# Moving the hardware loop of an expert pipeline by one pair, and splitting one expert's weight transfers

## The reference

```python
def moe_ffn(h, w_router, b_router, w_gu, b_gu, w_down, b_down):
    logits = t @ w_router + b_router                 # t: 256 tokens x 1024
    top_vals, top_idx = lax.top_k(logits, 4)         # 4 of 32 experts
    combine = scatter(softmax(top_vals))             # 256 x 32
    for e in range(32):
        gu = t @ w_gu[e] + b_gu[e]                   # 1024 x 2048 weights, 8 MB
        gate = min(gu[:, :1024], 7); lin = clip(gu[:, 1024:], -7, 7)
        act = gate * sigmoid(1.702 * gate) * (lin + 1)
        y = act @ w_down[e] + b_down[e]              # 1024 x 1024 weights, 4 MB
        out = out + combine[:, e:e+1] * y
    return out
```

## Time and profile before

| | |
|---|---|
| median of three runs | 1018.23 us |
| profiled execution | 1017.21 us |
| its span | 1015.3 us |
| PE busy | 957.4 us (94%) |
| DVE busy, ACT busy | 286.4 us, 134.3 us |
| moved by DMA | 419.63 MB, 413 GB/s over the span |
| PE waiting for gate/up weights | 42.9 us in 14 waits |

### The profile page before, as it was taken

How to read it: one execution, slowest core, us unless ns; L and a number is a source line. 1 busy time by engine, 2 the same in 40 slices (tenths; PEclk the granted TensorE clock), 3 DMA queues, 4 the chain that set the end, 5 groups by cost and what they waited for, 6 DMA issues and landing times.

```text
span 1015.3 us, 11590 instructions
## 1 busy us (share of the span) xinstructions
PE 957.4 (94%) x4807; PEld 416.8 (41%) x4807; DVE 286.4 (28%) x542; ACT 134.3 (13%) x215; POOL 10.2 (1%) x16
## 2 busy tenths in 40 slices
PE   8999999999998998989899898989899898999996
PEld 8978343434342432424243242424234342434332
DVE  5964522213121222122122112212211311222123
ACT  6825100000000010000001000000100000010002
POOL 0030000000000000000000000000000000000000
PEclk9999999999999998999999999999989998999998
DMA  9789999999999999999999999999999999999994
GB/s 322 274 374 378 387 424 423 427 429 427 430 431 430 431 432 431 425 430 429 432 431 434 431 428 426 431 432 434 432 432 429 426 429 431 434 432 432 421 424 197
DMA packets 28871, 419.63 MB, mean 413 GB/s; under 512 B 4276, under 2 KB 5960, under 8 KB 10888
## 3 DMA queue, kind: packets, MB, share of 16 engines
q1 hardware_dynamic: 28800, 419.16, 97.7%
q10 hardware_dynamic: 40, 0.01, 0.0%
HBM read 418.11 MB, written 1.05 MB: 413 GB/s over the span
## 4 chain that ended last, share of the span: by engine, by line
PE 57%; DMA 40%; DVE 2%; issue 0%; ACT 0%; SPq 0%; DVEq 0%
PE ps L1050 54%; DMA raw<-in_w_gu 37%; DMA raw<-in_w_down 4%; PE ps L1328 1%; PE ps L1383 1%; DVE woutl L774 1%; DVE biased L973 0%; PE ps L1057 0%; DMA cst<-in_consts 0%; PE ps L1225 0%; DVE acc L1029 0%; DVE outs L1032 0%; DVE uT L763 0%; DVE prT L796 0%; ACT junk L695 0%
## 5 line engine op out<-in xcount | busy, mean ns | idle before, releaser
L1050 PE MATMUL ps<-raw,xT 128*64 128x512 f32 x2032 | 472.2, 616 | 43.4 <-DMA raw<-in_w_gu 42.9
L1050 PEld LDWEIGHTS ps<-raw,xT 128*64 128x64 f32 x2032 | 143.2, 141 | 343.5 <-issue 282.7
L1050 PE MATMUL ps<-raw,actT 128*64 128x512 f32 x1024 | 232.3, 596 | 1.5 <-DMA raw<-in_w_down 1.3
L1050 PEld LDWEIGHTS ps<-raw,actT 128*64 128x64 f32 x1024 | 70.5, 137 | 135.3 <-issue 129.4
L973 DVE TENSOR_TENSOR biased<-ps,biasT 128x1024 f32<-128x1024 f32 x32 | 39.2, 1225 | 294.8 <-PE ps L1328 294.8
L651 ACT ACTIVATE gu<-ps 128x1024 f32<-128x1024 f32 x32 | 32.8, 1025 | 526.0 <-PE ps L1050 526.0
L990 DVE TENSOR_TENSOR acc<-ps,acc 128x512 f32<-128x512 f32 x60 | 38.8, 686 | 176.3 <-PE ps L1050 176.3
L874 DVE TENSOR_TENSOR xT<-ps,gT 128x512 f32<-128x512 f32 x32 | 22.1, 692 | 166.1 <-PE ps L1050 165.9
L1050 PE MATMUL ps<-ysc,dispT 64*128 64x512 f32 x256 | 65.5, 613 | 0.0
L1050 PEld LDWEIGHTS ps<-disp,h 128*128 128x128 f32 x512 | 58.4, 192 | 12.4 <-issue 12.2
L1050 PE MATMUL ps<-disp,h 128*128 128x128 f32 x512 | 61.7, 278 | 0.2 <-DVE disp L868 0.2
(11 more groups left out here) (163 smaller groups left out, 434.3 us busy)
## 6 DMA issues: line engine op xcount, KB each, us to landing
raw<-in_w_gu SPq DMA_DIRECT2D x55, 4096.0 KB, 33.4
raw<-in_w_down SPq DMA_DIRECT2D x62, 2048.0 KB, 31.4
raw<-in_w_gu SPq DMA_DIRECT2D x16, 2048.0 KB, 11.4
win<-in_w_in SPq DMA_DIRECT2D x15, 512.0 KB, 12.2
wout<-in_w_out SPq DMA_DIRECT2D x4, 1024.0 KB, 9.2
raw<-in_w_down SPq DMA_DIRECT2D x4, 1024.0 KB, 36.6
early<-in_w_gu SPq DMA_DIRECT2D x1, 2048.0 KB, 10.0
raw<-in_w_gu SPq DMA_DIRECT2D x2, 1024.0 KB, 6.0
```

The lines of the kernel that those rows point to most:

```text
L1050: return pe.matmul(out_, lhsT, rhs, start=start, stop=stop, skip_group_check=shared)
```

## The change

SP's and PE's loops run over other pairs. Pairs 0 and 1 are straight code, the loop runs four times over pairs 2 to 13, and pairs 14 and 15 are straight code. The call with `biases=True` is now that of pair 14, since pair 13 is in the loop. And pair 14 loads expert 30's gate/up weights by quarters of 2 MB, four transfers, where before it were two of 4 MB; the four semaphores of expert 1's quarters serve a second time (hence `uses=2`). The bytes and their order in the queue are as before.

```diff
 # SP
-            for third in range(3):
-                iteration(0, third)
-            with sp.Fori(1, triples) as j:
-                for third in range(3):
-                    iteration(j, third)
-            iteration(triples, 0)
-            iteration(triples, 1, small_next=last_loaded)
+            iteration(0, 0)
+            with sp.Fori(0, triples) as j:
+                iteration(j, 1)
+                iteration(j, 2)
+                iteration(j + 1, 0)
+            iteration(triples, 1, small=second_loaded, small_next=last_loaded)
             iteration(triples, 2, last=True)
 # PE
-            def gu_unit(half, c, s, count, pieces=None):
+            def gu_unit(half, c, s, count, pieces=None, uses=1):
...
-                        pe.wait_ge(pieces[c // 2], 16)
+                        pe.wait_ge(pieces[c // 2], 16 * uses)
...
-            def iteration(j, third, last, first=False, biases=False, pieces=None):
+            def iteration(j, third, last, first=False, biases=False, pieces=None, pieces_next=None, uses=1):
...
-                        gu_unit(0, k, buffer(j, third, 6 + k // 2), i + 1, third_loaded if first else None)
+                        gu_unit(0, k, buffer(j, third, 6 + k // 2), i + 1, pieces_next, uses)
...
-            iteration(None, 0, False, first=True, pieces=second_loaded)
+            iteration(None, 0, False, first=True, pieces=second_loaded, pieces_next=third_loaded)
             iteration(0, 0, False, pieces=fourth_loaded)
-            iteration(0, 1, False)
-            iteration(0, 2, False)
-            with pe.Fori(1, triples) as j:
-                for third in range(3):
-                    iteration(j, third, False)
-            iteration(triples, 0, False, biases=True)
-            iteration(triples, 1, False)
+            with pe.Fori(0, triples) as j:
+                iteration(j, 1, False)
+                iteration(j, 2, False)
+                iteration(j + 1, 0, False)
+            iteration(triples, 1, False, biases=True, pieces_next=second_loaded, uses=2)
             iteration(triples, 2, True, pieces=last_loaded)
```

## The result

The changed kernel took 1019.42 us, the median of 12 runs (1018.45 to 1022.41), beside 1017.76 us for the kernel before in 12 runs. The ratio is 1.0018, with a 95% interval of 1.0010 to 1.0025: 1.8 us slower, within the 0.3% that the prediction calls no change (the two medians lie 1.66 apart). The profiled execution took 1018.57 us with a span of 1016.6, where before it was 1017.21 and 1015.3. It is one of the shortest of the twelve, whose spans run from 1016.6 to 1020.6 with a median of 1017.6, so the 1.3 us between the two profiles need not be the 1.8 of the ratio.

A forecast was written before the change was run, and what follows sets the result against it. The prediction took weight transfers to bound the kernel until pair 14, then PE's own work. Its terms, +3.62 + 1.7 − 1.65 − 1.06 − 0.97 = +1.64, put the median of 1018.23 at 1019.9 us, range 1017.1 to 1022.4.

The forecast's parts named there:

- Biases, +3.62: Bias matmuls move from pair 13 to pair 14, ahead of its two short waits, and cost 3.62 us there.
- Low clock, +1.7: At pair 14's start, PE runs at low clock behind the longer wait and pays 1.7 us more.
- the 3.9 I gave: PE's wait ahead of pair 14 grows from 0.29 us to 3.9 us.
- the first rival: Long stretch of low clock at pair 14, price 3.0 us, and no gain from code: +3.9, 1022.1 us; chance 17%.
- Short waits taken up, −2.71: PE no longer waits 1.65 us for expert 30's second gate/up half, nor 1.06 us for its first down weights.
- Stream sooner, −0.97: Pairs 5 to 6 and 13 to 14 become loop turns without code loading, so weights come 0.97 us sooner.
- there I had 0.34: From pair 5 to 6, the distance falls from 58.78 to 58.44 us without code loading.
- Quarters, 0: Expert 30's gate/up weights in 2 MB transfers, issued one unit earlier at best, change the time by 0.
- Loop returns, 0: Returns at pairs 5, 8 and 11 are hidden behind waits for weights: cost 0, up to a few tenths without cover.
- the end on transfers: The end rests on transfers and PE takes up the biases: −0.97 to −1.58, 1016.7 to 1017.3 us; chance 8%.

## Why the prediction was right

Forecast were 1.64 us more; 1.8 were measured (1.0 to 2.5 by the interval). The mechanism held: the biases keep their price, a low clock comes behind the new wait, and the short waits take up part of both. That the sum came so close has luck in it. In the profile the sum was 0.34 too high, by the short waits; the terms of the clock and of the stream came near partly by chance, as the list shows; and beside the kernel with only the biases moved (1.0019) the stream's term cannot be seen in the changed kernel's time (1.0018). By its steps, against the profile:

- **Biases, +3.62.** Measured 16.56 − 11.24 − (5.35 − 3.65) = 3.62. Moving them alone gives the whole effect (1.0019).
- **Low clock, +1.7.** Measured 1.70 behind a wait of 3.39, and removed by filling that wait. The size was half luck: in the eight profiles in which pair 14 has a wait of over 3 us and no filler, four have the short stretch (5.24 or 5.35) and four the long (6.16 to 6.53). The wait was half a microsecond shorter than the 3.9 I gave, because I did not carry my own 0.63 us from the stream into it. In other executions the same term was 2.88 (6.53 − 3.65, with halves), as the first rival had it; that scatter may be part of why the ratio and the two profiles differ (1.8 and 1.3), which was not shown.
- **Short waits taken up, −2.71.** They took up 3.09: 3.62 + 1.70 − 2.23. The step was right and the size 0.38 short, because I read the brackets. These lines of the kernel before show it, the groups just ahead of the two waits of the earlier trace rows and the down group behind the first:

```profile
943.44 7.09 PE L1050 MATMUL ps<-raw,xT 128*64 128x512 f32 x32
...
959.09 3.60 PE L1050 MATMUL ps<-raw,actT 128*64 128x512 f32 x16
...
978.84 7.09 PE L1050 MATMUL ps<-raw,xT 128*64 128x512 f32 x32
```

  The last begins 8.14 us ahead of 986.98, and the same group in the changed kernel, which does not wait, 6.92 (981.42 to 988.34): the wait cost 1.22 and not 1.06. For the first, from 943.44 to the down group at 959.09 15.65 us pass, against 13.78 (947.90 to 961.68): 1.87 and not 1.65. A group's listed length holds the modelled end of its last matmul, which the next would overlap.
- **Stream sooner, −0.97.** In the profile pair 14 begins 0.87 sooner, but not by my steps. 0.24 of it are there at pair 13 and before. From pair 4 to 6 nothing was gained: 117.93 us against 117.83; there I had 0.34. The 0.63 from 13 to 14 appeared, but all three other kernels with the old loop had it too: I had taken a single late landing of the profiled execution for a price of the code. So the places were wrong, and that 0.87 came so near to 0.97 is luck. That less straight code makes the stream sooner on the whole is shown by the straight kernels; what the change gets of it is 0.6 to 0.8 us by the bytes, and between nothing and 1.2 us by the times.
- **Quarters, 0.** Shown both ways: 1.0000 when added alone, 1.0015 against 1.0018 when taken out. The wait goes and comes back at the transfers behind it.
- **Loop returns, 0.** No idle time past a landing at pairs 5, 8 and 11. Between 400 and 912 us, with the returns at pairs 8 and 11 inside, the queues of the changed kernel hold weights alone:

```profile
q1 hardware_dynamic: 10067, 220.70, 100.5%
```

  There is no row of an instruction queue: the loop's code was loaded in the first turn and not again. The Trainium skill ("Runtime: NRT & Kernel Launch", "Instruction fetch mechanics") says that a taken branch to a target outside the current two pages is held up until that page is fetched; this trace, with no packet in 512 us, does not agree for a loop of this size.

Of the rivals, the end on transfers was the wrong one for the changed kernel, and is the right one for the two looped kernels with the biases in pair 1.

## What to carry to other kernels

Where transfers bound the middle of a kernel and the compute engine has time over in each stage, small extra work is free as long as the waits for transfers behind it are longer than it, and what they can't take up comes out at the end. So it belongs early: here the same eight matmuls cost nothing that can be measured in pair 1, and 3.6 us by ratio in pair 14. When loops are moved, look at what sat in the straight stage that became looped and had to go elsewhere; that, and neither the loop nor the finer transfers, was all of the effect that the times can tell.

## What the runs showed of the hardware that I had not expected

- Useless matmuls in a wait can pay: 24 rows in 2.94 us kept the clock at 1.00 through the start of pair 14 and won 1.7 us there.
- The slow stretches go through a round over the pairs. In the changed kernel the first 16 rows took 5.35 and 5.35 us in pairs 6 and 7 and 3.65 in pair 12, then 6.12 in pair 13 and 5.35 in pair 14; in the other kernels the same lengths occur at other pairs. Which one falls on pair 14, where alone it counts, was worth 1.2 us between the changed kernel and the one with halves (6.53 − 5.35). The length of the wait alone does not set the price: with 24 filling matmuls pair 4 began at 327.33 behind 3.72 us of wait with 3.65, and without the biases at 326.10 behind 2.47 us of wait with 5.35.
- Straight code costs the weight stream: 12 straight pairs of PE code in place of a loop of three, 19 packets more, made the kernel 3.2 us slower with the biases in pair 1, and 2.3 us with them in pair 14 (1.0041 against 1.0018), though the packets are only 0.3 MB of 420. The weights are late in two pairs out of four, and by more than the missing bytes account for (3.7 us from pair 5 to pair 14 with the biases in pair 14, against 1.9 us). Why is open; it was not tried.
